# Forgetting heads: turned blocks rounded ahead of the next exponentials, and projection units on both sides of the slot behind the scores

## The chip, the cores and the metric

The kernel runs on one core of one Trainium2 chip. The metric is the device time in microseconds (us) of the whole program. TensorE is called PE here, VectorE DVE, ScalarE ACT, GpSimd POOL and SyncE SP, as in the profile. The profile is of one execution; the times are medians over several.

## The reference, cut to what matters

The program computes two transformer blocks and an output projection on 1024 tokens of width 1024. The change lies in the first block's mixers alone, in the part with eight "forgetting" attention heads of width 64:

```python
q_blocks = qh.reshape(B, H, nb, Q_BLOCK, Dh)            # 8 query blocks of 128 tokens
s = einsum('bhqd,bhkd->bhqk', qb, kh) + Fb[..., None] - F[:, :, None, :]
s = where(kpos[None, :] <= qpos[:, None], s, -inf)
p = softmax(s, axis=-1)
o = einsum('bhqk,bhkd->bhqd', p, vh)
```

`F` is a running sum of log-sigmoid gates. In front of these heads stands a gated linear attention (in two pairs of heads), whose last step is an RMS norm and a gate: `o * rsqrt(mean(o*o) + eps)`, times `silu(g)`.

## The kernel before, in words

Every large product is made of three matmuls on a value split in two: the high part (rounded) and the low part (the rest). A step written "hi" is the rounding, on ACT, and one written "lo" is the subtraction, on DVE or POOL.

`mixers` works through the forgetting heads in four pairs of heads. `pairs` runs the first three pairs in a loop (`body(i, True)`) and the last one behind it (`body(3, False)`). Each engine has a `body` of its own, and each goes through the same 32 slots: `slot // 16` is the head `h`, and `j = slot % 16` the place in it. Instructions of one engine run in the order written, and semaphores join the engines.

- Slots j = 0 to 7: `score` (L1237, matmuls L274 and L275 and the mask L1249) makes the scores of query block j on PE, in one of two areas of PSUM. DVE takes the negated row maxima (`maxes`, L992), ACT the exponentials and their row sum (`probs`, L742), DVE the reciprocal (`recip`, L997, one slot later), POOL scales the block (L594). The score of block j waits for the exponentials of block j - 2. The exponentials of block j wait for the scaling of block j - 2.
- Slots j = 4 to 7: the first four query blocks (group 0) are turned: `turn(i, h, 0, j - 4)` on PE (L1260, transposes), `turned` on ACT (L750, rounds the turned block) and `turned` on DVE (L1003, its low part). `times_v(i, h, 0, j - 5)` on PE (L1272 to L1274) multiplies the block before with the values, in slots 5 to 8. The last of them, in slot 8, is 128 columns wide.
- Slots j = 8 to 15: the other four query blocks (group 1) are turned and multiplied in the same way. `turn(i, h, 1, 0)` waits until all eight blocks of the head have been scaled.
- In the first three pairs PE also projects q, k and v of the next pair, cut into 48 units of three matmuls (`contract`, L390 to L392). `COUNT` says how many are made in each slot: 5 (in the second head 4) in slot j = 4, 5 in slot j = 8, 1 or 2 in most others. `FIRST_IN_SLOT` names the slots in which they stand in front of the turns. A run of eight units ends a piece; ACT copies it out (`piece`, `stage`, L715). Pieces end in both slots 4 and both slots 8.
- In the last pair there is nothing left to project but the pooling mixer: `contract_pool`, four units in each of the slots 2 to 9 of its first head, with ACT's `pool_copy` (L755) at the start of slots 4, 6, 8 and 10. Four small products (`mix_pool`) stand in its second head.

In front of the loop, ACT copies out the pieces of the first pair (`stage`), makes the inverse root of the linear attention's second pair (`rstd(1)`, L700 and L704, with two loads of a table), and rounds the values (`v_hi`). DVE makes the values' low parts (`v_lo`, L986) and then the gated outputs (`gated(1)`, L937 and L940, four instructions). Only then does DVE come to the first maxima.

Of the kernel before, what the change touches and what calls it, by code (L numbers as in the profile page):

```python
# [396 lines left out]
def mixers(core, mix, mix_at, gates):  # L397
# [6 lines left out]


    COUNT = [0, 0, 0, 3, 5, 1, 1, 1, 5, 1, 1, 1, 1, 1, 1, 2, 1, 1, 1, 1, 4, 1, 1, 1, 5, 2, 2, 2, 2, 0, 0, 0]
    FIRST_IN_SLOT = (4, 8)
    assert len(COUNT) == SLOTS and sum(COUNT) == 6 * KT
    units = [[(u // KT, u % KT) for u in range(sum(COUNT[:t]), sum(COUNT[:t + 1]))] for t in range(SLOTS)]
    ends = {t: p for t in range(SLOTS) for p, k in units[t] if k == KT - 1}  # L410
# [5 lines left out]
    with Phase(core, "fox") as ph, Phase(core, "gla") as pg, Phase(core, "gate") as pa, Phase(core, "in") as pi:  # L416
# [107 lines left out]
        with nc.Block() as block:  # L524
# [106 lines left out]
            def _(act):  # L631
# [131 lines left out]
                def body(i, more):  # L763
                    for slot in range(SLOTS):
                        h, j = slot // 16, slot % 16
                        if more and slot in (0, 3, 11):
                            ws.round_hi(act, ws.pair(i + 1, (0, 3, 11).index(slot)))
                        if not more and slot < 2:
                            ws.round_hi(act, ws.pool(slot))
                        if not more and slot in POOL_COPY:  # L770
                            pool_copy(POOL_COPY.index(slot))
                        if not more and slot in POOL_SCALE:
                            pool_scale(POOL_SCALE.index(slot))
                        if j < 8:
                            probs(i, h, j)
                        if more and j in FIRST_IN_SLOT:
                            piece(i + 1, slot)
                        if 4 <= j < 8:
                            turned(i, h, 0, j - 4)
                        if j >= 8:  # L780
                            for kt in second_turns[j]:
                                turned(i, h, 1, kt)
                        if not more:
                            continue
                        if j not in FIRST_IN_SLOT:
                            piece(i + 1, slot)
                        if slot in (24, 25):
                            q_hi(i + 1, slot - 24)
                        if slot in (26, 27):
                            k_hi(i + 1, slot - 26)  # L790
                        if slot == 30:
                            act.wait_ge(s["pv_done"], nth_pt(i, 1, 1, 3) + 3)
                            v_hi(i + 1, 0)
# [64 lines left out]
                act.wait_ge(s_am, 8)  # L858
                k_hi(0, 0)
                k_hi(0, 1)  # L860
                stage(0, 4, FIRST_BANKS[0])
                rstd(1)
                stage(0, 5, FIRST_BANKS[1])
                v_hi(0, 0)
                v_hi(0, 1)
# [3 lines left out]
            def _(dve):  # L869
# [233 lines left out]
                gate_rows(0, 1)  # L1103
                for z in range(2):
                    k_lo(0, z)
                for j in range(2):
                    v_lo(0, j)
                gated(1)
                pairs(dve, body)

            @block.tensor
            def _(pe):
# [164 lines left out]
                def body(i, more):  # L1277
# [3 lines left out]
                    for slot in range(SLOTS):  # L1281
                        h, j = slot // 16, slot % 16
# [3 lines left out]
                            score(i, h, j)  # L1286
                        if slot == 5:
                            pe.wait_ge(s["v_done"], 2 * i + 2)
                        if 4 < j <= 8:
                            times_v(i, h, 0, j - 5)  # L1290
                        if more and j in FIRST_IN_SLOT:
                            for p, k in units[slot]:
                                contract(i + 1, p, k)
                        if not more:
                            for m, k in pool_units.get(slot, ()):
                                contract_pool(m, k)
# [5 lines left out]
                        if j > 8:  # L1302
                            times_v(i, h, 1, j - 9)
                        if more:
                            if j not in FIRST_IN_SLOT:
                                for p, k in units[slot]:
                                    contract(i + 1, p, k)
                            if slot == 29:
                                turn_v(i + 1, 0)
                        elif slot in POOL_MIX:  # L1310
# [1792 lines left out]
```

## Time and profile before

| | us |
|---|---|
| median of 3 runs | 2346.45 (2344.78 to 2348.81) |
| the profiled execution, its own time | 2339.87 |
| its span in the trace | 2338.1 |
| PE busy (matmuls) | 2162.6, 92% of the span |
| DVE, ACT, POOL busy | 1238.0, 1015.1, 617.9 |
| mean granted clock of PE, share of full | 0.977 |

The span is what the trace shows between the first and the last instruction; 1.8 us of the execution's own time lie around it. In the trace the forgetting heads take the stretch from about 205 to 529 us: pair 0 begins at 205, pair 1 at 289, pair 2 at 368, pair 3 at 448 us, and its second head at 494 us. The profile's slices are 58 us wide, so this stage is slices 4 to 9 of 40. Within it PE is not quite full, and the rows below, read by slot, show the waits.

### The profile page before, as it was taken

To read this page: it belongs to the slowest core of one execution; us is meant where nothing else is said; L and a number is where in the kernel's file an instruction comes from. 1 tells how busy PE (TensorE), PEld (TensorE's weight loads), DVE (VectorE), ACT (ScalarE), POOL (GpSimd) and SP (SyncE) were. 2 spreads that over 40 slices of the span, in tenths; PEclk is the share of its full clock that TensorE was granted. 3 is DMA by queue.
4 is the path that set the end of the run, shared out by engine and by line. 5 is a ranking of instruction groups with operands and counts; after the bars stand their busy time and mean duration, and the time that the engine had idled before them with its cause. 6 is when DMAs were issued, how large, how long until landed. Compare 5 with 4: busy or idle time off the path is not lost. (4 is left out here: it accounts for less than half of the span.)

```text
span 2338.1 us, 28720 instructions
## 1 busy us (share of the span) xinstructions
PE 2162.6 (92%) x10344; PEld 1761.5 (75%) x10344; DVE 1238.0 (53%) x1650; ACT 1015.1 (43%) x1563; POOL 617.9 (26%) x387
## 2 busy tenths in 40 slices
PE   6998888887999999999999998999999999998678
PEld 5886777765878888888887877777878787786456
DVE  4645534435332222232445566777777777677553
ACT  4434434434321222221224354566666665656531
POOL 2212122254012222222344532322312222221040
PEclk9999999989999999999999999999999999999889
DMA  3100000004322121132424331101011110110052
GB/s 122 41 30 25 28 9 27 18 1 144 109 94 76 63 81 72 63 117 72 147 95 135 126 126 46 37 28 49 22 40 40 36 44 28 40 41 19 10 203 103
DMA packets 46690, 152.40 MB, mean 65 GB/s; under 512 B 6161, under 2 KB 6577, under 8 KB 46497
## 3 DMA queue, kind: packets, MB, share of 16 engines
q1 hardware_dynamic: 42768, 137.68, 16.6%
q0 software_dynamic: 3856, 13.86, 1.7%
q8 instruction: 40, 0.66, 0.1%
q14 instruction: 26, 0.20, 0.0%
HBM read 132.38 MB, written 18.88 MB: 65 GB/s over the span
## 5 line engine op out<-in xcount | busy, mean ns | idle before, releaser
L214 PE MATMUL psum<-h_hi,w_hi 128*128 128x512 f32 x704 | 274.1, 389 | 1.7 <-POOL w_lo L199 1.7
L215 PE MATMUL psum<-h_lo,w_hi 128*128 128x512 f32 x704 | 273.9, 389 | 0.0
L216 PE MATMUL psum<-h_hi,w_lo 128*128 128x512 f32 x704 | 273.9, 389 | 0.0
L2397 ACT ACTIVATE diff_probs<-psum,diff_neg_max 128x1280 f32<-128x1280 f32 x128 | 170.2, 1330 | 128.8 <-DVE diff_neg_max L2585 127.4
L2585 DVE TENSOR_REDUCE diff_neg_max<-psum 128x1 f32<-128x1280 f32 x128 | 189.5, 1487 | 56.8 <-PE psum L2053 56.5
L2110 PE MATMUL psum<-h_hi,w_hi 128*128 128x512 f32 x496 | 200.8, 405 | 16.4 <-POOL w_lo L2099 8.6
L1836 DVE SCALAR_TENSOR_TENSOR gu_ada_product<-gu_ada_w,gu_cond 128x1024 f32<-128x1024 f32 x48 | 92.1, 1919 | 214.5 <-DMA gu_ada_w<-in_ada_w 211.6
L199 POOL TENSOR_TENSOR w_lo<-w_whole,w_hi 128x1024 fp32r<-128x1024 f32 x44 | 105.4, 2397 | 367.4 <-ACT w_hi L190 367.4
L2111 PE MATMUL psum<-h_lo,w_hi 128*128 128x512 f32 x496 | 196.6, 396 | 0.0
L2112 PE MATMUL psum<-h_hi,w_lo 128*128 128x512 f32 x496 | 196.1, 395 | 0.0
L2302 POOL TENSOR_SCALAR diff_probs<-diff_probs,diff_recip 128x1280 f32<-128x1280 f32 x64 | 85.7, 1339 | 290.4 <-DVE diff_probs L2602 290.4
L1848 DVE TENSOR_TENSOR down_a_lo<-hid,down_a_hi 128x512 fp32r<-128x512 f32 x42 | 98.2, 2337 | 117.4 <-ACT down_a_hi L1756 115.5
L390 PE MATMUL psum<-h_hi,w_hi 128*128 128x512 f32 x368 | 151.8, 412 | 3.9 <-POOL w_lo L379 2.7
L190 ACT ACTIVATE w_hi<-w_whole 128x1024 fp32r<-128x1024 f32 x44 | 46.7, 1061 | 247.8 <-DMA w_whole<-in_w_gu 247.7
L214 PEld LDWEIGHTS psum<-h_hi,w_hi 128*128 128x128 f32 x704 | 132.2, 188 | 29.3 <-issue 2.1
L216 PEld LDWEIGHTS psum<-h_hi,w_lo 128*128 128x128 f32 x704 | 132.2, 188 | 27.4
L215 PEld LDWEIGHTS psum<-h_lo,w_hi 128*128 128x128 f32 x704 | 132.2, 188 | 27.4
L2052 PE MATMUL psum<-diff_k_hi_lo,diff_q_hi_twice 128*128 128x512 f32 (+1 forms) x384 | 141.4, 368 | 11.0 <-ACT diff_probs L2397 10.3
L392 PE MATMUL psum<-h_hi,w_lo 128*128 128x512 f32 x368 | 145.8, 396 | 0.0
L391 PE MATMUL psum<-h_lo,w_hi 128*128 128x512 f32 x368 | 145.4, 395 | 0.0
L1657 POOL TENSOR_TENSOR w_lo<-down_w_raw,w_hi 128x1024 fp32r<-128x1024 f32 x42 | 100.7, 2397 | 132.4 <-ACT w_hi L1754 132.4
L2053 PE MATMUL psum<-diff_k_hi_lo,diff_q_lo_twice 128*128 128x512 f32 (+1 forms) x384 | 130.9, 357 | 0.0
(377 smaller groups left out, 4892.9 us busy)
## 6 DMA issues: line engine op xcount, KB each, us to landing
w_whole<-in_w_gu SPq DMA_DIRECT2D x44, 512.0 KB, 3.4
down_w_raw<-in_w_down SPq DMA_DIRECT2D x44, 512.0 KB, 3.4
w_whole<-in_da_w_in SPq DMA_DIRECT2D x31, 512.0 KB, 3.6
gu_ada_w<-in_ada_w SPq DMA_DIRECT2D x24, 512.0 KB, 4.2
w_whole<-in_w_in SPq DMA_DIRECT2D x23, 512.0 KB, 3.4
diff_rope_half<-in_rope SPq DMA_DIRECT2D x17, 512.0 KB, 4.0
mix<-in_x SPq DMA_DIRECT2D x8, 512.0 KB, 8.6
wo_w_raw<-in_w_o SPq DMA_DIRECT2D x8, 512.0 KB, 3.5
```

Of the source, the lines that this page charges most:

```text
L214: pe.matmul(out, wh, rh, start=(k == 0), stop=False)
L215: pe.matmul(out, wh, rl, start=False, stop=False)
L216: last = pe.matmul(out, wl, rh, start=False, stop=(k == KT - 1))
L390: pe.matmul(out, wh, rh, start=(k == 0), stop=False)
L391: pe.matmul(out, wh, rl, start=False, stop=False)
L392: last = pe.matmul(out, wl, rh, start=False, stop=(k == KT - 1))
L2052: pe.matmul(out, self.q_hi[:, z, queries], self.k[:, z, keys], start=True, stop=False)
L2110: pe.matmul(out, wh, rh, start=(k == 0), stop=False)
L2111: pe.matmul(out, wh, rl, start=False, stop=False)
L2112: last = pe.matmul(out, wl, rh, start=False, stop=(k == KT - 1))
L2397: act.activation(dst, core.psum[:, 1536 * z:1536 * z + NKEY], ACT.Exp, bias=nm[:, qb % 2, z:z + 1], accum_out=rs[:, qb % 2, z:z + 1]).then ...
L2585: dve.tensor_reduce(nm[:, qb % 2, z:z + 1], core.psum[:, 1536 * z:1536 * z + NKEY], AX.X, ALU.max, negate=True).then_inc(s[f"max{z}"], 1)
```

## The change

Three edits, all in `mixers`:

1. ACT, slots j = 5 to 7, in all pairs: the rounding of the turned block (`turned(i, h, 0, j - 4)`) stands in front of the exponentials of block j instead of behind them. Slot 4 keeps its order. In slot 8 the copy of the piece stands behind the roundings of the turned blocks.
2. PE, slot j = 8 of the first three pairs: of the five units, two stand in front of `times_v` of the last turned block of group 0, and three behind the turns of group 1. Before, all five stood between the two. Slot 4 keeps its order.
3. In front of the loop, `rstd(1)` on ACT stands in front of `stage(0, 4)` instead of behind it, and `gated(1)` on DVE in front of the two `v_lo` instead of behind them.

No instruction is added or removed.

```diff
-    FIRST_IN_SLOT = (4, 8)
+
+    FIRST_IN_SLOT = {4: 5, 8: 2}
@@ ACT, body
+
+                        if 4 < j < 8:
+                            turned(i, h, 0, j - 4)
                         if j < 8:
                             probs(i, h, j)
-                        if more and j in FIRST_IN_SLOT:
-                            piece(i + 1, slot)
-                        if 4 <= j < 8:
-                            turned(i, h, 0, j - 4)
+                        if j == 4:
+                            if more:
+                                piece(i + 1, slot)
+                            turned(i, h, 0, 0)
                         if j >= 8:
                             for kt in second_turns[j]:
                                 turned(i, h, 1, kt)
                         if not more:
                             continue
-                        if j not in FIRST_IN_SLOT:
+                        if j != 4:
                             piece(i + 1, slot)
@@ ACT, in front of the loop
+                rstd(1)
                 stage(0, 4, FIRST_BANKS[0])
-                rstd(1)
                 stage(0, 5, FIRST_BANKS[1])
@@ DVE, in front of the loop
+                gated(1)
                 for j in range(2):
                     v_lo(0, j)
-                gated(1)
                 pairs(dve, body)
@@ PE, body
+                        if more and j in FIRST_IN_SLOT:
+                            for p, k in units[slot][:FIRST_IN_SLOT[j]]:
+                                contract(i + 1, p, k)
                         if 4 < j <= 8:
                             times_v(i, h, 0, j - 5)
-                        if more and j in FIRST_IN_SLOT:
-                            for p, k in units[slot]:
-                                contract(i + 1, p, k)
...
                         if more:
-                            if j not in FIRST_IN_SLOT:
-                                for p, k in units[slot]:
-                                    contract(i + 1, p, k)
+                            for p, k in units[slot][FIRST_IN_SLOT.get(j, 0):]:
+                                contract(i + 1, p, k)
```

## Rows read from the trace of the kernel before

**Rows 1.** Windows: stretch, us; busy of each engine (count); granted clock; DMA share; GB/s.

```profile
205.00:210.00 5.00, 0.99 (x6) 0.80 (x5) 4.58 (x4) 1.30 (x2) 2.55 (x1) 0.52 0.09 35
...
289.00:328.00 39.00, 33.45 (x172) 27.25 (x173) 15.11 (x31) 16.41 (x34) 13.08 (x11) 1.00 0.05 17
...
368.00:407.00 39.00, 33.62 (x166) 27.16 (x166) 15.11 (x31) 16.07 (x34) 13.05 (x11) 0.96 0.04 16
...
495.00:530.00 35.00, 26.38 (x109) 19.64 (x107) 14.70 (x31) 14.62 (x32) 15.62 (x17) 0.80 0.00 0
```

**Rows 2.** Waits of PE, 205 to 520 us: total us, times, longest.

```profile
PE psum L1272 <- DVE fox_pt_lo L1003: 19.9, 24, 2.1
PE psum L274 <- ACT fox_p_small L742: 10.2, 5, 5.8
PE psum L1260 <- DVE fox_pt_lo L1003: 6.9, 7, 1.1
```

**Rows 3.** Timeline of PE, slots 20 to 25 of pair 0: start, duration, instruction [idle before].

```profile
260.37 0.50 PE L1272 MATMUL psum<-fox_pt_hi,fox_v_hi 128*128 128x512 f32 x1 [0.71 <-DVE fox_pt_lo L1003]
...
261.16 0.49 PE L1260 MATMUL psum<-ident,fox_p_small 128*128 128x128 f32 x3
...
265.71 0.22 PE L1249 MATMUL psum<-fox_causal_r,fox_ident_r 128*128 128x128 f32 x1
266.27 0.39 PE L1272 MATMUL psum<-fox_pt_hi,fox_v_hi 128*128 128x256 f32 x1 [0.34 <-DVE fox_pt_lo L1003]
...
269.13 0.33 PE L1272 MATMUL psum<-fox_pt_hi,fox_v_hi 128*128 128x128 f32 x1 [1.44 <-DVE fox_pt_lo L1003]
...
269.52 0.44 PE L390 MATMUL psum<-h_hi,w_hi 128*128 128x512 f32 x1
...
272.99 1.03 PE L1260 MATMUL psum<-ident,fox_p_large 128*128 128x128 f32 x8
275.05 0.66 PE L1260 MATMUL psum<-ident,fox_p_large 128*128 128x128 f32 x4 [1.03 <-DVE fox_pt_lo L1003]
```

**Rows 4.** Timeline of ACT, slots 21 and 23 of pair 0.

```profile
261.22 0.91 ACT L742 ACTIVATE fox_p_large<-psum,fox_neg_max 128x768 f32<-128x768 f32 x1 [1.62 <-DVE fox_neg_max L992]
...
262.11 0.48 ACT L750 ACTIVATE fox_pt_hi<-psum 128x384 fp32r<-128x384 f32 x1
...
267.38 1.11 ACT L742 ACTIVATE fox_p_large<-psum,fox_neg_max 128x1024 f32<-128x1024 f32 x1 [1.62 <-DVE fox_neg_max L992]
...
268.48 0.27 ACT L750 ACTIVATE fox_pt_hi<-psum 128x128 fp32r<-128x128 f32 x1
```

**Rows 5.** Timelines of DVE and POOL, slots 21 to 24 of pair 0.

```profile
260.24 0.95 DVE L992 TENSOR_REDUCE fox_neg_max<-psum 128x1 f32<-128x768 f32 x1
...
266.13 1.21 DVE L992 TENSOR_REDUCE fox_neg_max<-psum 128x1 f32<-128x1024 f32 x1
...
268.99 0.15 DVE L997 RECIPROCAL fox_row_sum<-fox_row_sum 128x1 f32<-128x1 f32 x1
...
269.31 1.12 POOL L594 TENSOR_SCALAR fox_p_large<-fox_p_large,fox_row_sum 128x1024 f32<-128x1024 f32 x1 [0.72 <-DVE fox_row_sum L997]
```

**Rows 6.** Start of pair 0: line L940 (min/median/max ns), and timelines of ACT, DVE, PE.

```profile
L940 DVE TENSOR_TENSOR mix<-mix,gla_g_second x2: 692/1701/2710, 206.8 to 210.2; 128x512 f32<-128x512 f32 x2
...
199.01 1.28 ACT L704 ACT_TABLE_LOAD   x1
...
210.78 0.62 DVE L992 TENSOR_REDUCE fox_neg_max<-psum 128x1 f32<-128x128 f32 x2
...
211.32 0.37 ACT L742 ACTIVATE fox_p_small<-psum,fox_neg_max 128x128 f32<-128x128 f32 x1 [5.02 <-DVE fox_neg_max L992]
...
211.83 0.69 PE L274 MATMUL psum<-fox_k_hi_lo,fox_q_hi_twice 128*128 128x384 f32 x1 [5.83 <-ACT fox_p_small L742]
```

**Rows 7.** Timelines of ACT and PE, slots 7 and 8 of pair 3.

```profile
480.06 0.28 ACT L750 ACTIVATE fox_pt_hi<-psum 128x128 fp32r<-128x128 f32 x1 [0.94 <-PE psum L1260]
...
481.10 0.44 PE L390 MATMUL psum<-h_hi,w_hi 128*128 128x512 f32 x1
```

## The prediction, made before the changed kernel was run

> **What bounds the kernel now.** The page says that PE is busy 92% of the span, so only PE's idle time, or time that PE spends at the lower clock, can be won. The change touches one stage, some 324 us long. The windows by stage say how much is there: a first head of a pair keeps PE busy 33.5 of 39 us, the last head 26.4 of 35 us, and in the five microseconds in front of the first maxima PE works for only 1.0 us at 0.52 of its clock [rows 1]. The list of waits says for whom: 19.9 us for the low parts of turned blocks (L1003) in front of the products with the values, 6.9 us for the same in front of the next turns, and 10.2 us for exponentials, of which one wait alone is 5.8 us [rows 2]. Last I read one head slot by slot.
>
> **The head before.** In slots 21 to 24 the four waits of PE are 0.71, 0.34, 1.44 and 1.03 us [rows 3]. The other engines show why. DVE makes the maximum of block 5 from 260.24, ACT the exponentials from 261.22, then the rounding of the turned block from 262.11, though PE had turned it at 261.16 + 0.49 = 261.65 [rows 3 to 5]. Then comes DVE's low part, and only behind it DVE's next maximum. So maximum, exponentials, rounding and low part form one ring of about 3 us a slot, while PE has less than that to do. The last turn of the ring: maximum at 266.13, exponentials at 267.38, rounding at 268.48, PE at 269.13. Then five units (3.47 us from 269.52 to 272.99, 0.69 each), both turns of group 1 together, and a wait for the first low part of group 1, whose rounding came late because both turned blocks land at once with nothing for PE behind them. The same four waits stand in all six heads of the first three pairs, each within 0.03 us of these.
>
> **Edit 1 and 2, a head of the first three pairs.** I rebuild the slots with the same durations. Slot 21: the turned block is there at 261.65, so ACT rounds it from 261.69 and begins the exponentials at 262.08, 0.86 us later than before. The low part ends at 262.78 instead of 263.18. What waits for these exponentials is the score two slots on (264.6) and a reciprocal behind the next maximum (264.3); they end at 263.07, so the 0.86 us cost nothing, with 1.2 us of cover. Slot 22: PE has no wait in front of the product and runs 0.17 us ahead; the turned block is there at 264.08, and rounding and maximum (to 264.35) end together, so the exponentials start as before. Slot 23: the score ends 0.17 us earlier, near 265.76 (before: 265.71 + 0.22). PE's 0.34 us wait goes. The rounding lies inside the maximum (265.80 to 267.01), and the exponentials start at 267.05 instead of 267.38. The low part is ready at 267.4. Slot 24: PE reaches it at 266.86, makes two units (1.37 us) to 268.23, and finds the low part ready: the 1.44 us wait is gone.
>
> What is late next is the eighth block's scaling, for which the turns of group 1 wait. The exponentials end at 268.25, the reciprocal follows at once (before it stood behind a low part, at 268.99), and POOL starts 0.32 us behind it, as between 268.99 and 269.31, and takes 1.12 us [rows 5]: 268.29 + 0.32 + 1.12 = 269.73. PE stands ready at 268.62, so a **new wait of 1.17 us** appears in front of the turns at 269.79. Two turns take 0.8 us (0.9 behind a wait), three units 2.05 us, and slot 25 begins at 272.76 instead of 275.05 [rows 3]. The 1.03 us wait is gone too, since the three units lie over rounding and low part. That is 2.29 us a head. Behind it, ACT copies the piece after the roundings; q's rounding comes 1.1 us earlier instead of 2.3, but PE needs its first low part only 2 us after it is ready, so 1.1 us of slack remain. The load of the next weights starts from the end of the same piece; it shows up at most 0.5 us late on ACT, two slots ahead of its user on PE. Six heads at 2.27: **-13.6 us**. Bounds: with all four waits but the first gone, 0.34 + 1.44 + 1.03 = 2.81 a head (-16.9); with edit 1 worth nothing, PE would do its two units inside the 1.44 us, then wait for a scaling that ends at 269.31 + 1.12 = 270.43, and reach slot 25 near 273.4: 1.6 a head (-9.6).
>
> **Edit 3, the start.** ACT comes to the first exponentials at 211.32, 5.02 us after it was free, and PE sits idle for 5.83 us until 211.83 [rows 6]. Both wait for DVE, which makes the four instructions of `gated(1)` first and comes to the maxima at 210.78. One of them takes 2.71 us and its twin 0.69 [rows 6]; POOL was busy for 2.55 us in that window [rows 1]. Moved ahead, the four run from about 199.5 (the inverse roots come 1.26 us earlier with `rstd(1)`, whose inputs are ready since 188) and end near 202.4, with POOL idle, so at 0.7 each; the first `v_lo`, at 203.3, never notices. The maxima come at 205.9, but ACT first has a weight tile to round, to 206.2. Exponentials at 206.2, PE at 206.7: **-5.1 us**. The first projection unit then waits for POOL's tile (about 208.8), and PE is still at the lower clock to which it fell in that window (0.52) [rows 1]; if full clock returns as long after the restart as before, 4.9 us are left, and if it takes 3 us longer, 3.4. I take **-4.9** (-3.4 to -5.2).
>
> Row and skill on the moved `rstd(1)`: it holds two loads of the activation table. A load takes 1.28 us here [rows 6], and the next instruction starts right behind it. The Trainium skill ("ScalarE: Activation LUTs", What ACT_TABLE_LOAD costs) gives 1283 ns for the load, which agrees, and adds a drain of 1380 ns to each switch; as an estimate by that page, two switches would end the roots at 202.9 instead of 200.1, hold the last `stage` by 1.6 us and leave 3.3 us at the start. The trace shows no such drain. On the 2.71 us, the skill ("SBUF — State Buffer", Who interferes with whom) says that a DVE instruction with two SBUF inputs shares a read port with POOL and one of them blocks; the pair 2.71 and 0.69 agrees, and moving the step away from POOL's tile is what the rule would ask for.
>
> **The last pair.** In its first head ACT's new order puts the exponentials of blocks 5 to 7 behind turns that PE makes only after four units. Their own readers still have cover, but `pool_copy` stands behind them at the start of slots 6 and 8. In slot 8 the rounding is at 480.06 and PE's unit at 481.10 [rows 7]; with 1.1 us of exponentials put between, the copy ends at 481.93 and the unit starts at 481.98, +0.9. Slot 6 gives +0.15. Together **+1.0 us**. The second head has no units: there the ring alone sets the pace, its exponentials of block 7 start 0.7 us earlier and the scaling ends 1.05 us earlier: **-1.0 us**. Together 0, from -1.5 to +2.5.
>
> **The clock.** In the first head of pair 2 the clock is 0.96 over 39 us [rows 1]; half clock for 8% of it is 3.1 us, which costs 1.6. It fell during the waits that edits 1 and 2 mostly remove; I take half of it, **-0.8** (-1.6 to +2.8, should it fall at another place as at 0.52 in the start's window).
>
> **Sum**, on the profiled execution's own 2339.87 us: -13.6 - 4.9 + 0 - 0.8 = -19.3, so 2320.6. The median of the three runs lies 6.6 above that execution: 2346.45 - 19.3 = 2327.1, rounded **2327.0**. What follows the stage begins behind a barrier and its own loads, so it moves along as a whole.
>
> **Rivals.**
> - *Edit 1 does nothing* (the turned block isn't there before the maximum is, or the earlier low part frees nobody). For: it moves the last scaling by only 0.7 us. Against: in two of the three slots the block is turned before the maximum ends. Six heads at 1.6: -9.6 - 4.9 = -14.5, **2332.0**. Chance 0.17.
> - *The clock falls in the new wait.* The 1.17 us stand close behind the 0.71. For: pair 2 lost 1.6 us in such a head. Against: pair 1's first head had all four waits, longer in sum, and kept 1.00 [rows 1]. Six times 1.6 gives back 9.6: **2336.7**. Chance 0.09.
> - *Both, or later stages give it back*: within 0.2%. Chance 0.05, near 2343.
> - *Slower: the held exponentials are the path.* Place: ACT in slots 5 to 7, 24 times. If each hold of 0.86 us went to the next score instead of into cover, +20.6 against -14.5 would give **2352.6**. It decides from 14.5 / 24 = 0.6 us a hold. Against: the readers come 1.2 us after the end. Chance 0.04.
>
> **How the numbers follow.** The forecast case has 0.65 and its own range 2322 to 2331. The fast ends of all terms add up to 2321.2, the slow ends to 2338.7. I add a microsecond for the scatter of medians below and leave the corner of all slow ends out: 2320 to 2336. Changes under about 0.2% (4.7 us) can't be told from none. Faster 0.91, same 0.05, slower 0.04.
>
> **What would show it.** In the profile after: no wait for L1003 in front of the 128-column product of slots 8 and 24, a new wait of about 1.2 us on POOL's L594 in front of the eight turns, none in front of turn 2; L1003 falling from 27 us of PE's waits to under 10; the 5.8 us wait shrinking to under 1; L940 at 0.69 twice. Pair 1 beginning near 279.7 instead of 289.2. It would be wrong if ACT's exponentials of block 7 don't start earlier, or if the low clock shows in more stretches.

## The result, and the profile after

| | before | after |
|---|---|---|
| median, us | 2347.63 (2344.78 to 2353.03, 4 runs) | 2328.43 (2325.11 to 2328.76, 4 runs) |
| ratio | | 0.9909, 95% interval 0.989 to 0.9929 |
| the profiled execution, its own time | 2339.87 | 2328.16 |
| its span | 2338.1 | 2326.4 |
| first low part of k to last product of the last head, in that trace | 336.4 | 320.7 |

The medians differ by 19.2 us; the forecast was 2327.0 with a range of 2320 to 2336. The page of after, its row of busy times:

```profile
PE 2164.1 (93%) x10344; PEld 1766.0 (76%) x10344; DVE 1238.3 (53%) x1650; ACT 1016.5 (44%) x1563; POOL 618.4 (27%) x387
```

The two profiled executions differ by 11.7 us only. The last row of the table (called **the stage** below) shows where the rest is. The changed stage is 15.8 us shorter. The code in front of it, up to the first low part of k, came out 1.9 us longer in this trace of after. What lies behind it is the same in both kernels; counted from the next stage's first matmul (L1396, before L1393) to the end it came out 2.0 us longer, and the load in between 0.2 us. Over the traces of all kernels here this last part lasts 1799.9 to 1805.7 us, with no relation to the kernel. So a single trace is read inside the stage, and the medians tell the whole. The median of before lies 7.8 us above its profiled execution, whose 2339.87 us lie under all its other runs here (from 2340.51).

The waits of PE in the stage, after (total us, times, longest):

```profile
PE psum L1264 <- POOL fox_p_large L595: 9.0, 7, 1.9
PE psum L1276 <- DVE fox_pt_lo L1007: 6.9, 10, 0.9
PE psum L274 <- ACT fox_p_small L743: 5.5, 5, 1.4
...
PE psum L1264 <- DVE fox_pt_lo L1007: 0.9, 1, 0.9
PE psum L390 <- ACT mix L756: 0.7, 1, 0.7
```

To be compared with [rows 2]. Waits for low parts of turned blocks fell from 26.8 us to 6.9 + 0.9. The 5.8 us wait for exponentials at the start is 1.36 us. Two lines are as good as new: PE waits for POOL's scaling in front of the eight turns seven times, 9.0 us (six times 1.18 us, and 1.9 in the second head of the last pair, the only place where before had such a wait, of 0.4), and once for ACT's copy of the pooling mixer (0.7 us, in the last pair).

The same head as in [rows 3], slots 20 to 25 of pair 0, timeline of PE after (start, duration, instruction, idle before):

```profile
256.17 0.50 PE L1276 MATMUL psum<-fox_pt_hi,fox_v_hi 128*128 128x512 f32 x1 [0.70 <-DVE fox_pt_lo L1007]
...
261.35 0.33 PE L1276 MATMUL psum<-fox_pt_hi,fox_v_hi 128*128 128x256 f32 x1
...
263.94 0.22 PE L1276 MATMUL psum<-fox_pt_hi,fox_v_hi 128*128 128x128 f32 x1
...
265.56 1.09 PE L1264 MATMUL psum<-ident,fox_p_large 128*128 128x128 f32 x8 [1.18 <-POOL fox_p_large L595]
266.40 0.48 PE L390 MATMUL psum<-h_hi,w_hi 128*128 128x512 f32 x1
...
268.56 0.60 PE L1264 MATMUL psum<-ident,fox_p_large 128*128 128x128 f32 x4
```

Only the first of the four waits is left. The 256- and the 128-column product start with none, two units stand in front of the second of them, and the new wait of 1.18 us stands in front of the eight turns. From the first row to the last it is 268.56 - 256.17 = 12.39 us, against 275.05 - 260.37 = 14.68 before [rows 3]: 2.29 us gained. The waits shown differ by only 1.6 us. Most of the rest is what a wait costs beside its length. In front of a wait the tail of the last matmul stands alone; with work behind it the next matmul starts over it (the eight turns take 1.09 us, but the next matmul starts 0.84 us after them, 265.56 to 266.40). And the first 512-column matmul behind a wait is followed by the next after 0.33 us (256.17 to 256.50), one in a running row after 0.23 us, with 0.39 us of length. That makes, as an estimate from these rows, 0.16 + 0.10 us for each wait, and there are two waits fewer.

ACT and DVE/POOL in the same slots, after:

```profile
257.50 0.49 ACT L751 ACTIVATE fox_pt_hi<-psum 128x384 fp32r<-128x384 f32 x1 [2.11 <-PE psum L1264]
257.88 0.90 ACT L743 ACTIVATE fox_p_large<-psum,fox_neg_max 128x768 f32<-128x768 f32 x1
...
262.06 0.28 ACT L751 ACTIVATE fox_pt_hi<-psum 128x128 fp32r<-128x128 f32 x1 [0.77 <-PE psum L1264]
262.81 1.12 ACT L743 ACTIVATE fox_p_large<-psum,fox_neg_max 128x1024 f32<-128x1024 f32 x1 [0.47 <-DVE fox_neg_max L996]
...
261.55 1.23 DVE L996 TENSOR_REDUCE fox_neg_max<-psum 128x1 f32<-128x1024 f32 x1 [0.85 <-PE psum L1253]
...
264.05 0.16 DVE L1001 RECIPROCAL fox_row_sum<-fox_row_sum 128x1 f32<-128x1 f32 x1 [1.01 <-ACT fox_p_large L743]
...
264.38 1.12 POOL L595 TENSOR_SCALAR fox_p_large<-fox_p_large,fox_row_sum 128x1024 f32<-128x1024 f32 x1 [0.34 <-DVE fox_row_sum L1001]
```

ACT now rounds the 128-column block at 262.06, inside DVE's maximum (261.55 to 262.78), and starts the exponentials 0.03 us behind it. Before, the exponentials started 0.04 us behind the maximum too, but 7.01 us after the first row of [rows 3] (267.38 - 260.37), now 6.64 us. The reciprocal of block 7 follows 0.12 us behind its exponentials (it stood behind a low part before [rows 5]), and POOL starts 0.33 us behind it. That scaling ends at 265.50, and PE turns at 265.56: this is the chain that bounds slot 24 now.

### The profile page after: what moved, and what is told of

Same layout as the page of the kernel before. It is cut to its first block and busy times, and to the rows that moved or that the text cites. A ratio compares the mean times of both kernels' runs of the same rounds, so it can differ in the third digit from the quotient of the medians.

```text
span 2326.4 us, 28720 instructions
## 1 busy us (share of the span) xinstructions
PE 2164.1 (93%) x10344; PEld 1766.0 (76%) x10344; DVE 1238.3 (53%) x1650; ACT 1016.5 (44%) x1563; POOL 618.4 (27%) x387
```

## Experiments

The columns below: *stage* as in the table above; *head to head* is the time from the eight turns in the first head of pair 0 to those in its second head, which holds every slot once and is free of what happens at the start of a pair (37.37 us before, 35.02 after). Medians stand beside those of before on the same chip.

| kernel | median, us (before beside it) | ratio, 95% | stage | head to head |
|---|---|---|---|---|
| start_only | 2341.34 (2345.85) | 0.9973, 0.9955 to 0.9991 | 334.3 | 37.42 |
| split_only | 2337.58 (2345.85) | 0.9964, 0.9954 to 0.9974 | 327.5 | 35.75 |
| swap_only | 2333.65 (2345.85) | 0.9952, 0.9936 to 0.9968 | 327.0 | 35.50 |
| three_ahead | 2322.89 (2345.85) | 0.9907, 0.9891 to 0.9924 | 312.8 | 34.35 |
| after_again | 2324.23 (2344.09) | 0.9912, 0.989 to 0.9933 | 317.9 | 35.00 |
| last_pair_old | 2325.40 (2344.09) | 0.9927, 0.99 to 0.9953 | 314.2 | 35.00 |
| four_and_three | 2314.84 (2344.09) | 0.9869, 0.9852 to 0.9887 | 309.7 | 33.61 |
| before_again | 2343.87 (one run) | | 338.0 | 37.37 |
| one_ahead | 2335.41 (one run; 2347.57) | | 329.9 | 37.26 |
| four_ahead | 2318.80 (one run; 2347.57) | | 312.1 | 34.21 |
| gated_only | 2329.00 (one run; 2347.57) | | 317.8 | 35.01 |

### Edit 3 alone

```diff
                 k_hi(0, 1)
-                stage(0, 4, FIRST_BANKS[0])
                 rstd(1)
+                stage(0, 4, FIRST_BANKS[0])
...
                     k_lo(0, z)
+                gated(1)
                 for j in range(2):
                     v_lo(0, j)
-                gated(1)
```

> The kernel before with edit 3 alone (inverse roots and gated outputs of the linear attention moved ahead; the slots as before). Theory, each edit has its own place: the wait of 5.8 us in front of the third score becomes about 1.4 us, that score comes 4.9 us earlier counted from the low parts of k, and whatever the lower clock takes after the restart comes off that: 3.4 to 5.1 us in the stage, a median near 2343. The six heads keep their four waits of 0.71, 0.34, 1.44 and 1.03 us. Rival, the start's gain only shifts a wait for POOL's weight tile: then the first projection unit starts no more than 2 us earlier and the median is unchanged.

Timeline of PE, start_only, where [rows 6] has the 5.83 us wait:

```profile
208.95 0.69 PE L274 MATMUL psum<-fox_k_hi_lo,fox_q_hi_twice 128*128 128x384 f32 x1 [1.35 <-ACT fox_p_small L742]
```

From the first low part of k to this matmul it is 14.79 us, and 19.68 before: 4.9 us, as expected. But the eight turns of that head come only 3.65 us earlier than in the profiled execution of before (and 4.4 us earlier than in before_again), so 1.2 us are missing against the first. What they are is told with the clock below. The medians differ by 4.5 us, and the interval of the ratio reaches from 2 to 11 us: alone, the edit is just clear of no change.

### Edit 2 alone

```diff
-    FIRST_IN_SLOT = (4, 8)
+    FIRST_IN_SLOT = {4: 5, 8: 2}
@@ PE, body
+                        if more and j in FIRST_IN_SLOT:
+                            for p, k in units[slot][:FIRST_IN_SLOT[j]]:
+                                contract(i + 1, p, k)
                         if 4 < j <= 8:
                             times_v(i, h, 0, j - 5)
...
+                            for p, k in units[slot][FIRST_IN_SLOT.get(j, 0):]:
+                                contract(i + 1, p, k)
```

This kernel also has ACT's new order in slot 8, the copy of the piece behind the roundings, which the list of the change has under edit 1. The kernel of the next section lacks it.

> The kernel before with edit 2 alone (two units ahead of the last product of group 0 and three behind the turns of group 1; ACT keeps exponentials ahead of the turned block). Theory, worked out as the rival in which edit 1 does nothing: the units fill the 1.44 us wait, the 1.03 us wait goes, and a wait of about 0.9 us appears for the scaling of block 7, which still ends 1.4 us behind the last reciprocal's issue as before: 1.6 us a head, 9.6 us in six heads, a median near 2338. Last pair unchanged. Rival, edit 1 carries the gain: under 0.5 us a head.

Timeline of PE, split_only, slots 20 to 24 of pair 0, all its waits:

```profile
263.61 0.50 PE L1274 MATMUL psum<-fox_pt_hi,fox_v_hi 128*128 128x512 f32 x1 [0.71 <-DVE fox_pt_lo L1005]
...
269.52 0.39 PE L1274 MATMUL psum<-fox_pt_hi,fox_v_hi 128*128 128x256 f32 x1 [0.34 <-DVE fox_pt_lo L1005]
...
273.74 1.09 PE L1262 MATMUL psum<-ident,fox_p_large 128*128 128x128 f32 x8 [0.81 <-POOL fox_p_large L595]
```

The waits of 1.44 and 1.03 us are gone, that of 0.34 us stays, and a wait of 0.81 us on the scaling is there without edit 1 too. A head is 1.62 us shorter.

### Edit 1 alone

```diff
+                        if 4 < j < 8:
+                            turned(i, h, 0, j - 4)
                         if j < 8:
                             probs(i, h, j)
...
-                        if 4 <= j < 8:
-                            turned(i, h, 0, j - 4)
+                        if j == 4:
+                            turned(i, h, 0, 0)
```

> The kernel before with edit 1 alone (turned block rounded ahead of the exponentials in slots 5 to 7; all five units stay between the last product of group 0 and the turns). Theory: the 0.34 us wait goes, the 1.44 us wait shrinks to about 0.55 us and comes earlier, the turns find the blocks scaled, the 1.03 us wait stays: 1.65 us a head, 9.9 us in six heads; the last pair's first head loses 0.9 us in front of the units of slot 8, its second gains 0.3 to 1. A median near 2338. With the split's 1.6 this is 3.25 a head if the two added up; both together gave 2.29, so they overlap by about 1 us, the new wait on the scaling. Rival, the held exponentials are the path: each head as long as before or up to 2.6 us longer, a median of 2348 to 2363.

Timeline of PE, swap_only, slots 20 to 24 of pair 0, all its waits:

```profile
261.44 0.50 PE L1274 MATMUL psum<-fox_pt_hi,fox_v_hi 128*128 128x512 f32 x1 [0.71 <-DVE fox_pt_lo L1005]
...
268.36 0.33 PE L1274 MATMUL psum<-fox_pt_hi,fox_v_hi 128*128 128x128 f32 x1 [0.36 <-DVE fox_pt_lo L1005]
...
274.28 0.66 PE L1262 MATMUL psum<-ident,fox_p_large 128*128 128x128 f32 x4 [1.03 <-DVE fox_pt_lo L1005]
```

The 0.34 us wait is gone, that of 1.44 us is 0.36 us, and the 1.03 us wait in front of turn 2 stays, since nothing stands between the turns. A head is 1.87 us shorter, where 1.65 us were expected with a remaining wait of 0.55 us; the median, 2333.65, lies under the expected 2338.

What follows from the two: alone they give 1.62 and 1.87 us a head, 3.49 together, but the kernel with both gives 2.35. Some 1.1 us are the same microseconds: both take away the 1.44 us wait (edit 1 alone 1.08 us of it, edit 2 alone all). That is why the sum had to be made by rebuilding the slots with both edits and not by adding edits. The rival "edit 1 does nothing" falls: with edit 2 there, edit 1 still takes 37.37 - 1.62 - 35.02 = 0.73 us off each head, four to five microseconds in all.

### What bounds slot 24 now: units in front of the last product

The text of after with another number of units in front in slots 8 and 24, the rest of the five behind the turns:

```diff
-    FIRST_IN_SLOT = {4: 5, 8: 2}
+    FIRST_IN_SLOT = {4: 5, 8: 3}
```

> The changed kernel with three units ahead of the last product and two behind the turns, in place of two and three. Theory, what is late now is the scaling of block 7 and nothing else: the third unit (0.69 us) fills that wait, which falls from 1.18 to about 0.5 us, and slot 9 begins 0.65 us earlier, if the two units left still cover rounding and low part of the first turned block, which I expect by a hair (0 to 0.1 us of wait): 2.9 us a head against the kernel before, 3.5 to 4 us less than the changed kernel in all, a median near 2324.5. Rival, the wait is fixed by the product in front of it (low part late): the wait stays 1.18 us and the low part of the first turned block is missed by 0.7 us, a median of 2328.

```diff
-    FIRST_IN_SLOT = {4: 5, 8: 2}
+    FIRST_IN_SLOT = {4: 5, 8: 4}
```

> The changed kernel with four units ahead and one behind. Theory: no wait on the scaling any more; the turns start 0.18 us later than with three; the one unit left doesn't cover the 2.0 us from the start of the turns to the first low part, so a wait of about 0.4 us on the low part comes back in front of the third turn (1.03 us before the change); head to head 34.25 us, within 0.15 of three ahead. Rival, more units ahead always pay: 33.7 us.

```diff
-    FIRST_IN_SLOT = {4: 5, 8: 2}
+    FIRST_IN_SLOT = {4: 5, 8: 1}
```

> The changed kernel with one unit ahead and four behind in slots 8 and 24. Theory, the turns of group 1 start when block 7 is scaled, whatever stands in front of them: the wait on the scaling grows from 1.18 to 1.86 us, the turns start at the same time, and slot 9 begins 0.68 us later: from the eight turns of pair 0's first head to those of its second 35.7 us (35.0 with two ahead, 34.35 with three), and 4.1 us in six heads. Rival, the product ahead of the turns sets them: then it waits for its low part now (0.3 us or more) and the turns start later than with two.

Timeline of PE, three_ahead, the eight turns of the first head (1.18 us of wait in after):

```profile
228.81 1.09 PE L1264 MATMUL psum<-ident,fox_p_large 128*128 128x128 f32 x8 [0.50 <-POOL fox_p_large L595]
```

Timeline of PE, four_ahead, the turns of group 1 in the second head:

```profile
265.34 0.66 PE L1264 MATMUL psum<-ident,fox_p_large 128*128 128x128 f32 x4 [0.28 <-DVE fox_pt_lo L1007]
```

Timeline of PE, one_ahead, the second head of pair 0, and under it its windows there (stretch, us, busy time of the engines, granted clock, DMA share, GB/s):

```profile
265.62 1.09 PE L1264 MATMUL psum<-ident,fox_p_large 128*128 128x128 f32 x8 [1.85 <-POOL fox_p_large L595]
...
262.00:265.60 3.60, 1.78 (x10) 1.36 (x9) 1.96 (x5) 1.48 (x3) 2.13 (x2) 1.00 0.00 0
265.60:271.00 5.40, 5.38 (x21) 4.38 (x22) 1.29 (x2) 1.09 (x2) 0.00 (x0) 0.68 0.00 0
271.00:276.00 5.00, 5.00 (x28) 4.14 (x27) 3.27 (x5) 4.83 (x7) 0.00 (x0) 1.00 0.01 2
```

Each unit moved in front takes its 0.69 us out of the wait on the scaling: 1.85, 1.18, 0.50 us and, with four, none. With three a head is 0.67 us shorter than with two. The fourth brings 0.14 us only, because a wait of 0.28 to 0.36 us for the first low part comes back in front of turn 2: one unit does not cover the rounding and the low part. So two chains meet there, the scaling in front and the low part behind. Of the splits tried, four in front and one behind is the shortest, by 0.14 us a head, and three and two is next; the change as made, two and three, leaves 0.8 us a head.

With one unit the wait came out as expected, 1.85 us, but not the time. The head of pair 2, from turns to turns, is 35.69 us, the 0.68 us expected above after's 35.0. Those of pairs 0 and 1 are 37.26 and 37.31. The last rows show why: in the second head of pair 0 the granted clock is 1.00 in front of the turns, 0.68 in the 5.4 us behind them, and 1.00 again. Matmuls of a unit then come 0.43 us apart instead of 0.23. Behind the 1.85 us wait the clock fell to its lower level in five of the six heads (0.63, 0.68, 0.61, 0.58 and 0.59 over the next 4 to 5 us, 1.00 in the first head of pair 2), and it costs 37.26 - 35.69 = 1.57 us in pair 0 and 1.62 in pair 1. Behind the 1.18 us wait of after it fell in none of six (1.00 in all six windows of 4 us behind the turns), nor in any of the 18 heads with this wait in after_again, last_pair_old and gated_only, whose heads take 35.00 to 35.02 us in every pair. The 1.85 us wait is there in one trace only. The expectation was wrong by this. The rival "the clock falls in the new wait" was wrong for after and right one unit further.

### Edit 3 without its ACT part

```diff
-                rstd(1)
                 stage(0, 4, FIRST_BANKS[0])
+                rstd(1)
                 stage(0, 5, FIRST_BANKS[1])
```

> The changed kernel with the inverse roots (rstd) at their old place, gated outputs ahead of the values' low parts as in the change. Theory: DVE waits for the roots until 1.3 us later, the gated outputs end 1.2 us later and hold the first low part of the values by 0.5 us; counted from the first low part of k the third score comes at 15.3 us (14.79 with both moved, 19.67 with neither), so the four DVE instructions carry 4.4 of the 4.9 us. Rival, both moves are needed: 17 us or more.

Timeline of DVE, gated_only, and the matmul that PE waits for:

```profile
203.39 0.75 DVE L941 SCALAR_TENSOR_TENSOR mix<-gla_o,cols_sb,gla_rstd 128x512 f32<-128x512 f32 x1 [5.56 <-ACT gla_rstd L705]
...
210.00 0.69 PE L274 MATMUL psum<-fox_k_hi_lo,fox_q_hi_twice 128*128 128x384 f32 x1 [1.36 <-ACT fox_p_small L743]
```

DVE waits 5.56 us for the inverse roots instead of 4.25, and the third score comes 15.42 us after the first low part of k instead of 14.79. So 4.3 of the 4.9 us come from DVE's order alone, and 0.6 from moving the roots.

### The last pair, and the kernel before and after again

```diff
-                        if 4 < j < 8:
+                        if 4 < j < 8 and (more or h):
                             turned(i, h, 0, j - 4)
                         if j < 8:
                             probs(i, h, j)
+                        if 4 < j < 8 and not (more or h):
+                            turned(i, h, 0, j - 4)
```

> The changed kernel, but in the first head of the last pair ACT keeps the exponentials ahead of the turned block in slots 5 to 7. Theory, there the new order only puts exponentials ahead of the copies that PE's pooling units wait for: the wait of 0.70 us for the copy (L755) in front of the units of slot 8 goes, and with it a tenth or two in slot 6; the stage is 0.85 us shorter, which the median can't show. Rival, the new order pays there too: the wait of 0.69 us in front of the 128-column product stays and turns into a later start of the second head.

The kernels before and after, unchanged, gave the traces to compare with and the medians of that chip:

> The kernel before, unchanged, for a second profile. The profile on record ran in 2339.87 us, where its runs otherwise took 2343 to 2353. Theory, the 4 to 6 us between them lie in other stages (projections behind the heads, waits for weights) and not in the forgetting heads: counted from the first low part of k to the last product of the last head, 336.4 us here as there, within 1 us, with the same four waits in every head. Rival, they lie in the heads, as more stretches at the lower clock: 338 us or more, with the clock under 1.00 at the start of pair 1 or 2 as well.

> The changed kernel, unchanged, for a second profile and more times on the chip of the others. Theory, waits and slots repeat to 0.02 us and only the stretches at the lower clock move: 320.8 us for the stage, plus or minus 1.5 us. In the first profile the clock fell at the start of pairs 1, 2 and 3. A median of 2326 to 2329. Rival, the falls belong to the new order: again at all three starts.

The waits of the heads repeated in both, but both expectations failed in the length of the stage, and the rivals' signs came. In before_again the stage took 338.0 us, 1.5 more than in the profile on record, and the lower clock shows at the start of pair 1 too (294 to 298 us). Of the 4.0 us between the two executions, the other 2.5 lie in front of the stage. In after_again the stage took 317.9 us, under the 319.3 allowed, and the median is 2324.23 (beside 2344.09 for before on that chip). The clock fell again at the starts of pairs 1, 2 and 3. But last_pair_old, which has the same order there, has no fall at the starts of pairs 1 and 2, so these falls don't belong to the new order.

Slots 7 and 8 of pair 3, first head, after: timelines of ACT and PE, where [rows 7] has 480.06 and 481.10:

```profile
466.07 0.28 ACT L751 ACTIVATE fox_pt_hi<-psum 128x128 fp32r<-128x128 f32 x1 [3.03 <-PE psum L1264]
466.24 1.11 ACT L743 ACTIVATE fox_p_large<-psum,fox_neg_max 128x1024 f32<-128x1024 f32 x1
...
467.33 0.60 ACT L756 ACTIVATE mix<-psum 128x512 f32<-128x512 f32 x1
...
467.98 0.50 PE L390 MATMUL psum<-h_hi,w_hi 128*128 128x512 f32 x1 [0.70 <-ACT mix L756]
```

Waits of PE from 440 us to the end of slot 8 in last_pair_old, all of them:

```profile
PE psum L1278 <- DVE fox_pt_lo L1009: 1.7, 3, 0.7
```

The copy (467.33) stands behind 1.11 us of exponentials, and PE's unit waits 0.70 us for it; from rounding to unit it is 1.91 us, 1.04 before [rows 7]. With the old order there is no such wait. From the 384-column matmul of slot 6's score to the eight turns, at full clock throughout, it is 12.92 and 12.94 us in the two traces of before, 14.18 and 14.20 in those of after, and 12.97 in last_pair_old. All thirteen traces fall into these two groups, 12.92 to 12.98 us with the old order in this head (six) and 14.14 to 14.20 with the new one (seven). So the new order costs **1.26 us** in this head (0.85 was expected), and undoing it there gives it back. The wait of 0.69 us in front of the 128-column product stays, as the rival said, but the later start that it named doesn't come. In the whole program that could not be told: 2325.40 beside 2324.23, with overlapping intervals.

### A version that beats both

Three units in front in slots 8, 20 and 24 and four in slot 4, ACT's first rounding in front of its piece, and the old order in the last pair's first head:

```diff
-    FIRST_IN_SLOT = {4: 5, 8: 2}
+    FIRST_IN_SLOT = {4: 4, 8: 3, 20: 3, 24: 3}
@@ ACT, body
                         if j == 4:
-                            if more:
-                                piece(i + 1, slot)
                             turned(i, h, 0, 0)
...
-                        if j != 4:
-                            piece(i + 1, slot)
+                        piece(i + 1, slot)
@@ PE, body
-                        if more and j in FIRST_IN_SLOT:
-                            for p, k in units[slot][:FIRST_IN_SLOT[j]]:
+                        if more and slot in FIRST_IN_SLOT:
+                            for p, k in units[slot][:FIRST_IN_SLOT[slot]]:
...
```

(The lines of last_pair_old are in this kernel too and cut here, and so is PE's second lookup, which goes by the slot as well.)

> Three units ahead in slots 8 and 24 and two behind; and in slots 4 and 20 the last unit behind the turn, with ACT's copy of the piece behind the rounding; and the old order in the last pair's first head. Theory, the first wait of a head (0.71 us for the low part of the first turned block) is of the same kind as the one in slot 8: turned one unit earlier, the low part is ready when the next score ends, and the wait is gone, 0.7 us a head. With the third unit (0.68 us a head) and the last pair's 0.85 us: 9 us less than the changed kernel, a median near 2319, and about 3.65 us a head against the kernel before. Rival, the ring of maximum, exponentials, rounding and low part takes its time back in slots 21 to 23, so that a wait of 0.5 us or more stands in one of them: a median of 2323.

Timeline of PE, four_and_three, slots 20 to 24 of pair 0:

```profile
252.63 0.50 PE L1275 MATMUL psum<-fox_pt_hi,fox_v_hi 128*128 128x512 f32 x1
...
262.01 1.09 PE L1263 MATMUL psum<-ident,fox_p_large 128*128 128x128 f32 x8 [0.50 <-POOL fox_p_large L595]
```

With a unit behind the first turn, the product of slot 21 (252.63) has no wait; the 0.70 us that after still has is gone, and only 0.50 us on the scaling is left. A head is 33.61 us, 3.76 us under before (3.65 were expected). The median, 2314.84 where 2319 was expected, is 29.3 us under that of before and 9.4 under that of after_again on the same chip. Four units in front in slots 8 and 24 were not tried together with this.

## Why the prediction was right, and where it was not

- **The head, 2.29 us, new wait 1.17.** Measured 2.29 and 1.18 [rows 3 to 5, and the rows of after]; in all six heads the wait is 1.18, and head to head gives 2.35. The step that did it is the rebuild of the slots with the durations of before, with the other chain (exponentials, reciprocal, 0.32 us, scaling) looked up before the gain was counted. The terms of the edits alone held too (1.6 for edit 2, measured 1.62).
- **The start, -4.9 us.** The maxima came 13.75 us after the first low part of k, as forecast (205.9 - 192.15), L940 took 0.69 us twice, and the third score moved by 4.9 (5.1 was forecast; ACT waited 0.23 us for the maxima). What differs from the forecast in this pair of traces is the clock behind it. Rows of DVE, ACT and PE at the start of pair 0, after, and the units of PE there before:

```profile
203.70 0.69 DVE L944 TENSOR_TENSOR mix<-mix,gla_g_second 128x512 f32<-128x512 f32 x1
...
207.77 0.61 DVE L996 TENSOR_REDUCE fox_neg_max<-psum 128x1 f32<-128x128 f32 x2
...
199.57 1.28 ACT L705 ACT_TABLE_LOAD   x1
200.86 1.15 ACT L705 ACTIVATE gla_rstd<-gla_rstd 128x512 f32<-128x512 f32 x2
...
208.30 0.37 ACT L743 ACTIVATE fox_p_small<-psum,fox_neg_max 128x128 f32<-128x128 f32 x1 [0.23 <-DVE fox_neg_max L996]
...
208.81 0.69 PE L274 MATMUL psum<-fox_k_hi_lo,fox_q_hi_twice 128*128 128x384 f32 x1 [1.36 <-ACT fox_p_small L743]
...
213.46 0.63 PE L390 MATMUL psum<-h_hi,w_hi 128*128 128x512 f32 x1
...
215.62 0.45 PE L390 MATMUL psum<-h_hi,w_hi 128*128 128x512 f32 x1
```

```profile
213.81 0.73 PE L390 MATMUL psum<-h_hi,w_hi 128*128 128x512 f32 x1
...
215.19 0.50 PE L390 MATMUL psum<-h_hi,w_hi 128*128 128x512 f32 x1
```

  After, matmuls of units still take 0.63 us at 213.46 and 0.45 at 215.62, with the restart at 208.81: full clock returned some 6 us behind it. Before, the restart was at 211.83 and the unit at 215.19 takes 0.50 us already: about 3.4 us. So some 1.2 us are missing in this pair of traces, and the term is -3.7: inside its bounds (-3.4 to -5.2), at the end named for "3 us longer". But that is scatter and not a property of the new order. The same program in after_again:

```profile
209.05 0.69 PE L274 MATMUL psum<-fox_k_hi_lo,fox_q_hi_twice 128*128 128x384 f32 x1 [1.35 <-ACT fox_p_small L743]
...
212.41 0.42 PE L390 MATMUL psum<-h_hi,w_hi 128*128 128x512 f32 x1
```

  Here full clock is back 3.4 us behind the restart, and in before_again it took 5.1 us (restart at 214.28, first short matmul at 219.36). From the first low part of k to the first product with the values (slot 5 of pair 0) it is 30.8 and 31.6 us in the two traces of before and 27.1 and 25.9 us in those of after: -3.7 us in the one pair, -5.7 in the other. Over the four traces with the old start it is 31.2 us on average, over the seven with the whole of edit 3 and slot 4 as in after it is 26.5: -4.7. So -4.9 was right on average. Pair 1 begins at 282.70 in after and at 281.60 in after_again, which is 280.8 and 279.5 on the time of before; 279.7 was forecast. The wait on the exponentials is 1.36 us, not under 1: PE stopped 0.4 us earlier than in the trace of before, counted from the first low part of k, since the two scores in front of the wait ran at full clock here (256 columns in 0.33 us, in 0.50 before).
- **The table load.** 199.57 + 1.28 = 200.85, and the next instruction starts at 200.86: no drain behind a load, as in [rows 6], and none in front of it (the instruction before ends at 199.55). The estimate by the Trainium skill ("ScalarE: Activation LUTs", What ACT_TABLE_LOAD costs), that the start would bring only 3.3 us, is out: 4.9 were measured at the third score. The roots ended at 202.01, which is 200.1 on the time of before, where that estimate had 202.9. On the shared port, the trace agrees again with the Trainium skill ("SBUF — State Buffer", Who interferes with whom): with POOL idle both instructions take 0.69 us where one took 2.71.
- **The last pair.** The first head cost 1.26 us instead of 1.0: slot 8 0.87 (1.91 - 1.04) as forecast, slot 6 0.24 in place of 0.15, the remaining 0.15 between them not traced to one row. The second head gained 0.9 (turns of the first head to the end of the stage 44.70 and 44.71 before, 43.81 and 43.64 after) against 1.0. But PE runs at the lower clock for part of that head in every trace. The four traces with the old order there take 44.58 to 44.71 us, the nine with the new one 42.42 to 43.83. So the gain is shown, and its size only as 0.8 to 2.3 us.
- **The clock, -0.8 us: the term that the two profiled executions contradict, with +1.5 us.** Its reading of before holds: the fall in pair 2's first head, on which it rested, is in both traces of before, behind the same wait of 1.43 us. First before_again, then the trace of before:

```profile
392.96 0.33 PE L1272 MATMUL psum<-fox_pt_hi,fox_v_hi 128*128 128x128 f32 x1 [1.43 <-DVE fox_pt_lo L1003]
...
394.58 0.63 PE L390 MATMUL psum<-h_hi,w_hi 128*128 128x512 f32 x1
```

```profile
390.70 0.63 PE L390 MATMUL psum<-h_hi,w_hi 128*128 128x512 f32 x1
```

  Some 4 us at the lower clock follow in both. start_only has these waits too and no such fall, and in the 42 heads of the seven traces with both edits and two or more units in front there is none. What the term left out is the starts of the pairs (only its range, to +2.8, allowed for a fall elsewhere). The trace of before has no fall at the starts of pairs 1 and 2, and after has one at each. First two units of pair 1 in after, and the first in last_pair_old, the same wait in front:

```profile
286.62 0.74 PE L390 MATMUL psum<-h_hi,w_hi 128*128 128x512 f32 x1 [0.65 <-POOL w_lo L379]
...
288.00 0.63 PE L390 MATMUL psum<-h_hi,w_hi 128*128 128x512 f32 x1
```

```profile
285.14 0.50 PE L390 MATMUL psum<-h_hi,w_hi 128*128 128x512 f32 x1 [0.64 <-POOL w_lo L379]
```

  The wait is 0.65 and 0.64 us; in one trace the unit takes 0.74 us and the next comes 1.38 us behind, in the other it runs at full clock. From the last turns of a pair to those of the next it is 40.48 and 40.38 us in after, 39.86 and 39.92 in after_again, 38.93 and 38.90 in last_pair_old: such a fall costs 0.9 to 1.6 us here. Of the two starts, none is hit in before and last_pair_old, one in before_again, three_ahead and gated_only, both in the other eight traces, with the old order and with the new. What decides it stays open. The two falls of after in pairs 1 and 2, less the one of before, leave 1.5 us on the other side of the account. The forecast's sign of being wrong, "the low clock shows in more stretches", so came true for this pair (six stretches in the stage, five before), but before_again has six too.
- **The account of the stage**, on the two profiled executions: start -3.7, six heads -14.0 (2.29 + 5 x 2.35), last pair +1.5 (0.2 of it ahead of slot 6) and -0.9, clock +1.5: -15.6, where the traces show -15.8. The forecast for the same was -19.3. The difference is 1.2 at the start and 2.3 at the clock. The second pair of traces gives 338.0 - 317.9 = -20.0, by the same marks start -5.7, six heads -14.0, last pair +0.2, clock -0.5. The medians give -19.2 and -19.9. So the six heads repeat and the clock's part moves by some microseconds from trace to trace. The forecast's size is right for the median (2328.43, forecast 2327.0) and was 7.6 us off for the profiled execution (2328.16, forecast 2320.6); that the median was hit to 1.4 us is in part luck.
- **Rivals.** "Edit 1 does nothing" is refuted by swap_only and by after against split_only. "The clock falls in the new wait" didn't occur at 1.18 us and did at 1.85. That later stages give the time back (near 2343) is ruled out by the medians. "The held exponentials are the path": PE's waits for exponentials in after are all for `fox_p_small`, the first four blocks, and none is for the held ones of blocks 5 to 7; the place where a hold did cost is the last pair, by way of the copy behind it.

## What to carry to other kernels

Two edits that shorten the same wait are summed by rebuilding the slot with both and looking up the chain that is late next, not by adding each alone (1.62 + 1.87 gave 2.35). Filler work on the busy engine is to be divided between the waits in front and behind so that each just covers its chain, and then tried one unit to each side: here 0.67 us a head lay one unit away on the one side, and 2.25 us a head would have been lost on the other. When an engine's instruction is moved ahead, look at what stands behind the one that it overtakes: the cost in the last pair came from a copy two places further on.

## What the runs showed of the hardware that was not expected

- A wait of PE of 1.85 us was followed by the lower clock in five of six heads (one trace), one of 1.18 us in none of 24 (four traces). One of 1.42 to 1.44 us was followed by it in two of 18 heads (three traces), both times in the first head of pair 2. At the start of a pair the same waits (1.1 and 0.65 us, a few matmuls apart) were followed by it in some traces and not in others. A fall of some 4 us cost 0.9 to 1.6 us, about as much as the wait itself.
- After the idle time at the start, full clock came back some 3 to 6 us behind PE's restart, and not after the same time in two traces of one program: about 3.4 and 5.1 us in before, 6 and 3.4 in after. So a restart that is 4.9 us earlier showed as 3.7 us further on in one pair of traces and as 5.7 in the other.
- A wait costs more than its length: with the 1.6 us of waits that went, 2.3 us of time went in the head shown, which comes to some 0.3 us more for each of the two waits that are gone.
- The same code behind the stage took from 1799.9 to 1805.7 us, so that one trace's span can't show a gain of some microseconds, while the same stretch between two named instructions repeats within 0.02 us (head to head 35.00 to 35.02 in all twelve pairs of after, after_again, last_pair_old and gated_only).
